# Recurrence of a hybrid block: a reordered step, and level matrices as 128x128 block diagonals

## The reference, cut to what matters

```python
def step(s, inp):                     # s: 64x64 state per direction and head
    r_t, w_t, k_t, v_t, aa_t, bb_t = inp
    sa = jnp.einsum('dbhij,dbhj->dbhi', s, aa_t)
    s = s * w_t[..., None, :] + sa[..., :, None] * bb_t[..., None, :] \
        + v_t[..., :, None] * k_t[..., None, :]
    y_t = jnp.einsum('dbhij,dbhj->dbhi', s, r_t)
    return s, y_t
```

## Time and profile before

| what | us |
|---|---|
| median of three runs (2741.93 to 2745.86) | 2744.94 |
| the profiled execution | 2746.3 |
| its span | 2744.5 |
| TensorE busy in the span | 2602.0 (95%) |
| VectorE, ScalarE, GpSimd busy | 960.9, 563.6, 148.3 |
| the recurrence, in the span | 1420.2 to 1667.4 |

### The profile page before, as it was taken

One profiled execution on the slowest core, in us unless ns is written; L12 is line 12 of the kernel. 1 busy time (PEld: TensorE's weight loads), 2 busy tenths in 40 slices (PEclk: granted clock), 3 DMA queues, 4 the chain that ended last, 5 costly groups with the idle time before them and its releaser, 6 DMA issues.

```text
span 2744.5 us, 42039 instructions
## 1 busy us (share of the span) xinstructions
PE 2602.0 (95%) x18006; PEld 1724.2 (63%) x18006; DVE 960.9 (35%) x1993; ACT 563.6 (21%) x1071; POOL 148.3 (5%) x125
## 2 busy tenths in 40 slices
PE   7999999998999999999998789799999999999998
PEld 6867878887885887888877777433333333333333
DVE  1773463312377254313576653411111111111112
ACT  2100233301100223301333323111111111111112
POOL 0050000000041000000012220000000000000000
PEclk9999999999999999999999999899999999999999
DMA  6645323343554432335400002599999999999995
GB/s 228 215 167 201 114 101 123 123 154 127 183 209 160 165 111 92 123 138 194 173 14 3 4 4 93 236 426 428 428 428 428 428 428 428 428 428 428 428 428 252
DMA packets 135044, 636.06 MB, mean 232 GB/s; under 512 B 5136, under 2 KB 5408, under 8 KB 109152
## 3 DMA queue, kind: packets, MB, share of 16 engines
q1 hardware_dynamic: 133904, 629.78, 57.8%
q0 software_dynamic: 1008, 4.30, 0.4%
HBM read 633.01 MB, written 1.05 MB: 231 GB/s over the span
## 4 chain that ended last, share of the span: by engine, by line
PE 92%; DVE 4%; ACT 3%; issue 1%; DMA 1%; SPq 0%; ACTq 0%; DVEq 0%
PE bank L265 25%; PE bank L2540 17%; PE bank L2568 9%; PE bank L455 6%; PE bank L1402 5%; PE bank L477 4%; PE bank L286 4%; PE bank L1337 4%; PE bank L2502 2%; PE bank L2531 2%; PE bank L2488 2%; PE bank L1624 1%; PE bank L353 1%; PE bank L2560 1%; ACT hidT L2650 1%
## 5 line engine op out<-in xcount | busy, mean ns | idle before, releaser
L265 PE MATMUL bank<-hT,ring 128*128 128x256 f32 x3136 | 694.7, 382 | 13.0 <-DVE hT L706 13.0
L265 PEld LDWEIGHTS bank<-hT,ring 128*128 128x128 f32 x3136 | 596.3, 191 | 106.8 <-DVE hT L706 14.8
L2540 PE MATMUL bank<-ring,hsel 128*64 128x512 f32 x2112 | 462.0, 595 | 0.0
L2540 PEld LDWEIGHTS bank<-ring,hsel 128*64 128x64 f32 x2112 | 149.0, 137 | 311.5 <-issue 311.5
L2812 DVE TENSOR_SCALAR glu<-bank 128x256 f32<-128x256 f32 x66 | 28.0, 425 | 761.0 <-PE bank L2540 757.7
L2568 PE MATMUL bank<-ring,hidT 128*64 128x512 f32 x1024 | 226.8, 595 | 22.0 <-ACT hidT L2650 22.0
L1402 PE MATMUL bank<-ring 64*64 64x64 f32 (+1 forms) x5760 | 179.9, 230 | 42.1 <-DVE ring L2136 19.0
L739 DVE SCALAR_TENSOR_TENSOR a_buf<-v_pad,par,a_buf 128x256 f32<-128x256 f32 x480 | 215.8, 532 | 0.0
L1402 PEld LDWEIGHTS bank<-ring 64*64 64x64 f32 x5760 | 168.1, 141 | 54.4 <-issue 19.7
L2568 PEld LDWEIGHTS bank<-ring,hidT 128*64 128x64 f32 x1024 | 70.7, 137 | 156.0 <-issue 127.9
L2641 ACT ACTIVATE sig<-glu 128x256 f32<-128x256 f32 x66 | 27.5, 417 | 463.6 <-DVE glu L2812 463.6
(11 more groups left out here) (421 smaller groups left out, 2491.3 us busy)
## 6 DMA issues: line engine op xcount, KB each, us to landing
ring<-in_w SPq DMA_DIRECT2D x196, 2048.0 KB, 15.5
ring<-in_w_in SPq DMA_DIRECT2D x66, 2048.0 KB, 7.9
ring<-in_w_ada SPq DMA_DIRECT2D x12, 2048.0 KB, 8.1
ring<-in_w_ret_out SPq DMA_DIRECT2D x8, 2048.0 KB, 7.9
ring<-in_w_out SPq DMA_DIRECT2D x6, 2048.0 KB, 8.0
ring<-in_w_conv_out SPq DMA_DIRECT2D x4, 2048.0 KB, 8.5
ring<-in_w_attn_out SPq DMA_DIRECT2D x4, 2048.0 KB, 7.8
extra<-in_w SPq DMA_DIRECT2D x2, 2048.0 KB, 25.3
```

What stands on the lines that cost most here:

```text
L265: mm = nc.tensor.matmul(out[:, j, :], w[:, k, col + j * P:col + (j + 1) * P], rhs[:, k, :], start=(k == 0), stop=(k == DC - 1))
L2540: mm = nc.tensor.matmul(half(flat[4 + b], side), g["hsel"][:, 2 * (j % 2) + k, j // 2, :], w[:, at:at + UNIT], start=False, stop=(j == 3 a ...
```

## The change

In `mixer_memory`, `cut` gets two buffers, each with a 128x128 matrix per direction and pair; MP loses its second half to a new MQ. GpSimd zeroes `cut` once, and then writes each level in four pieces: two directions, two halves of 64 partitions, each into its own block (for the backward direction the off-diagonal one). TensorE's first product of a level, `t1`, is one product of 128 rows instead of two halves. X0 is no longer formed by VectorE from MP: X1 is turned through the identity into PSUM (`turn_x1`), X0's updates accumulate there, and ScalarE copies X0 out after each level (`keep_x0`). The pairs and starts of the next turn (`front`) come ahead of the state products. The token turns go ahead of levels 1 to 3, the other products between `t1` and the second products (`between`). The number of waits falls: TensorE waits for both directions at once. The loras of the latent half go ahead of turn 0 and behind turns' ends. The expert stage only takes its counters from other, spent semaphores.

```diff
-    g["cut"] = flat[:, at:at + LEVELS * DN * C2].rearrange("p (k n w) -> p k n w", k=LEVELS, n=DN)
+    g["cut"] = flat[:, at:at + 2 * DN * P].rearrange("p (k n w) -> p k n w", k=2, n=DN)
...
                 if k == 0:
                     pool.wait_ge(g["pairs_out"].sem, g["pairs_out"].at(turn, d + 1))
-                nc.gpsimd.tensor_tensor(g["cut"][:, k, d * NC:(d + 1) * NC, :], g["MP"][:, d * NC:(d + 1) * NC, 0:C2],
-                                        row(mask[:, k, d, :], NC), ALU.mult).then_inc(
-                    g["levels_cut"].sem, g["levels_cut"].one())
+                elif k > 1:
+                    pool.wait_ge(g["t_done"].sem, g["t_done"].at(turn, 2 * (k - 1)))
+                for lo in (0, 64):
+                    to = 64 - lo if d else lo
+                    nc.gpsimd.tensor_tensor(
+                        g["cut"][lo:lo + 64, k % 2, d * NC:(d + 1) * NC, to:to + 64],
+                        g["MP"][lo:lo + 64, d * NC:(d + 1) * NC, :],
+                        mask[lo:lo + 64, k, d, :].unsqueeze(1).to_broadcast([64, NC, C2]), ALU.mult).then_inc(
+                        g["levels_cut"].sem, g["levels_cut"].one())
+    pool.wait_ge(g["p_out"].sem, g["p_out"].at(None, CTX_CHUNKS + 20))
+    nc.gpsimd.memset(g["cut"][:, :, :, :], 0.0).then_inc(g["wf_zero"].sem, g["wf_zero"].one())
...
+        def turn_x1(d, c):
+            for lo in (0, 64):
+                to = 64 - lo if d else lo
+                mm = nc.tensor.matmul(chunk(4 + d, c)[to:to + 64], g["XX"][lo:lo + 64, d, 1, c, :],
+                                      ident[lo:lo + 64, lo:lo + 64], start=c == 0, stop=False, skip_group_check=True)
+            return mm
+
+        def t1(k):
+            return lambda d, c: nc.tensor.matmul(chunk(d, c), g["cut"][:, k % 2, d * NC + c, :], g["XX"][:, d, 1, c, :],
+                                                 start=True, stop=True)
+
+        def d1(d, c):
+            return halves(chunk(2 + d, c), g["XX"][:, d, 0, c, :], g["T1"][:, d * NC + c, :], turned=d == 1)
+
+        def d0(k):
+            return lambda d, c: halves(chunk(4 + d, c), g["T1"][:, d * NC + c, :], g["XX"][:, d, 0, c, :],
+                                       False, k == LEVELS - 1)
...
+        def between(k):
+
+            if k == 0:
...
+                both_ways(keys, "pairs_done")
+            if k == 1:
...
+                if lat:
+                    both_ways(more, "more_done")
+                if turn == 2:
+                    lora(1, 3, 6)
+            if k == 2:
...
+                both_ways(g0_state, "g0_done", True)
+            if k == 3:
...
+                both_ways(g0_keys, "g0_done")
+            if k == 4:
...
+                if keep_state:
+                    both_ways(state_keys)
+                if lat:
+                    both_ways(out_state, "y_step", True)
+
+        for k in range(LEVELS):
+
+            if k == 0:
+                pe.wait_ge(g["x_ready"].sem, g["x_ready"].at(turn, 2))
+                both_ways(turn_x1, "x1_turned")
+            else:
...
+                if k < 4:
+                    both_ways(by_token(("sV", "sB", "sK")[k - 1]))
+                pe.wait_ge(g["x_next"].sem, g["x_next"].at(turn, 2 * k))
+            pe.wait_ge(g["levels_cut"].sem, g["levels_cut"].at(turn, 4 * k + 4))
+            both_ways(t1(k), "t_done")
+            between(k)
+            pe.wait_ge(g["t_out"].sem, g["t_out"].at(turn, 2 * k + 2))
...
+            if k < LEVELS - 1:
+                both_ways(d1, "d_done")
+            both_ways(d0(k), "x0_done")
+
+        pe.wait_ge(g["x0_out"].sem, g["x0_out"].at(turn, 2 * LEVELS))
+        both_ways(u, "u_done")
         if turn == 0:
...
+            key_sums(1, 2)
         if turn == 1:
...
+            lora(1, 2, 2)
+        if keep_state and turn != STEPS - 1:
+            front(turn + 1)
+        pe.wait_ge(g["u_out"].sem, g["u_out"].at(turn, 2))
         if keep_state:
...
+            both_ways(state_rates, "s_done")
...
         if lat:
...
+            both_ways(out_keys)
+            both_ways(out_rates, "y_step")
+        if turn == STEPS - 1:
+            front(turn + 1)
```

ScalarE and VectorE follow:

```diff
+        def keep_x0(k):
+            for d in range(DIRS):
+                act.wait_ge(g["x0_done"].sem, g["x0_done"].at(turn, 2 * k + d + 1))
+                nc.scalar.activation(g["XX"][:, d, 0].rearrange("p c w -> p (c w)"), flat[4 + d][:, 0:NC * C2], ACT.Copy).then_inc(
+                    g["x0_out"].sem, g["x0_out"].one())
+
         for k in range(LEVELS):
+            if k:
+                keep_x0(k - 1)
             for d in range(DIRS):
...
+    def start_inverse(turn):
+
+        dve.wait_ge(g["first_done"].sem, g["first_done"].at(turn, 1))
         for d in range(DIRS):
...
+            v.tensor_tensor(g["MP"][:, d * NC:(d + 1) * NC, :], flat[d][:, 0:NC * C2].rearrange("p (n w) -> p n w", n=NC),
+                            row(keep[:, d, 0:C2], NC), ALU.mult).then_inc(g["pairs_out"].sem, g["pairs_out"].one())
+        for d in range(DIRS):
+            x = g["XX"][:, d, 1]
+            v.tensor_tensor(x, flat[d][:, NC * C2:2 * NC * C2].rearrange("p (n w) -> p n w", n=NC), row(first[:, d, :], NC),
+                            ALU.mult).then_inc(g["starts_set"].sem, g["starts_set"].one())
+            dve.wait_ge(g["starts_set"].sem, g["starts_set"].at(turn, d + 1))
+            v.tensor_tensor(x, x, row(g["mc"]("eye"), NC), ALU.add).then_inc(g["x_ready"].sem, g["x_ready"].one())
...
+        start_inverse(turn)
+        if turn:
+            add_state(turn - 1)
...
+                    v.tensor_tensor(x, x, flat[2 + d][:, 0:NC * C2], ALU.add).then_inc(g["x_next"].sem, g["x_next"].one())
```

More of the change, by code:

```diff
@@ L1404, in halves, with both_ways, chunk, front @@
         return mm
-    def both_ways(product, last, signal, per_direction=False):
-        for c in range(last + 1):
+    def both_ways(product, signal=None, last_only=False):
+        for c in range(NC):
             for d in range(DIRS):
                 mm = product(d, c)
-                if signal and c == last and (d or per_direction):
+                if signal and c == NC - 1 and (d or not last_only):
                     mm.then_inc(g[signal].sem, g[signal].one())
[L1414 to L1432, removed]
+    ident = g["c"]("ident")
+    def chunk(bank, c, at=0):
+        return flat[bank][:, at + c * C2:at + (c + 1) * C2]
+    def front(turn):
+        def pairs(d, c):
+            dc = d * NC + c
+            return halves(chunk(d, c), g["sB"][:, dc, :], g["sA"][:, dc, 0:C2], turned=d == 1)
         def first(d, c):
             dc = d * NC + c
-            return halves(flat[4 + d][:, c * C2:(c + 1) * C2], g["sA"][:, dc, 0:C2], g["sB"][:, dc, :], turned=d == 1)
-        def by_token(name, bank, at):
+            return halves(chunk(d, c, NC * C2), g["sA"][:, dc, 0:C2], g["sB"][:, dc, :], turned=d == 1)
+        pe.wait_ge(g["staged"].sem, g["staged"].at(turn, 1))
+        both_ways(pairs)
+        both_ways(first, "first_done", True)
+    def step(turn):
+        lat, i = turn >= STEPS, turn % STEPS
+        state = g["ST"][turn % 2]
+        keep_state = turn < 2 * STEPS - 1
+        new_col = C2 * (1 + turn % 2)
+        def by_token(name):
             def product(d, c):
@@ L1537, in step @@
-        for d in range(DIRS):
-            pe.wait_ge(g["x_next"].sem, g["x_next"].at(turn, 2 * (LEVELS - 1) + d + 1))
-            for c in range(NC):
-                mm = halves(flat[d][:, c * C2:(c + 1) * C2], g["XX"][:, d, 0, c, :], g["G0"][:, d * NC + c, :])
-            mm.then_inc(g["u_done"].sem, g["u_done"].one())
+                    mm = nc.tensor.matmul(chunk(d, c, NC * C2)[to:to + 64], g[name][lo:lo + 64, d * NC + c, :],
+                                          ident[lo:lo + 64, lo:lo + 64], start=True, stop=True)
@@ L1559, in mixer_tensor @@
+    pe.wait_ge(g["p_out"].sem, g["p_out"].at(None, CTX_CHUNKS + 20))
+    pe.wait_ge(g["lora_out"].sem, g["lora_out"].at(None, 4))
+    lora(1, 0, 2)
+    lora(1, 1, 6)
+    front(0)
+    g["first_done"].n = 0
+    for turn in each_turn(g, 2 * STEPS, SCAN):
+        step(turn)
     pe.wait_ge(g["gates_ready"].sem, g["gates_ready"].at(None, 1))
@@ L1753, in aside @@
             key_exp(1)
-        if n in (14, 15):
-            take_lora(1, 2, 4, n - 14)
-        if n in (18, 19):
-            take_lora(1, 3, 4, n - 18)
+        if n == 23:
+            for part in range(2):
+                take_lora(1, 3, 6, part)
         if 25 <= n < 37:
@@ L2166, in step, with add_state @@
+    def add_state(turn):
         for d in range(DIRS):
@@ L2168, in step, with new_state @@
             h = slice(d * NC, (d + 1) * NC)
-            ins = v.tensor_tensor(g["sum"][:, h, :], old[:, h, :],
+            ins = v.tensor_tensor(g["sum"][:, h, :], g["ST"][turn % 2][:, h, :],
                                   flat[6 + d][:, 0:NC * C2].rearrange("p (n w) -> p n w", n=NC), ALU.add)
-        ins.then_inc(steps.sem, steps.one())
-        dve.wait_ge(steps.sem, steps.now(i))
```

(17 more changed lines are left out.)

388 lines of the change are left out of this document (162 added, 226 removed).

## The result

The changed kernel takes 2760.85 us (median of 4 runs, 2759.64 to 2764.93), the kernel before beside it on the same chip 2745.33 us (4 runs, 2741.93 to 2745.86). The ratio is 1.0062, 95% interval 1.0044 to 1.0079: slower by 15.5 us, where 2766 was forecast. The profiled execution has a span of 2759.0 us, against 2744.5.

The account below looks back on a forecast made before the run. TensorE bounds the kernel, and the 247.2 us recurrence moves the end one for one. Products +34, shape switches +8, d1 -15 give +27 us of work; less 6 of better covered waits, +21 on 2744.9: 2766 us, range 2741 to 2783.

Parts of the forecast that it names:

- The sign and the size: Recurrence stage +21 us, passed on in full to the end: 2766 us; slower by more than noise, chance 0.69.
- Rival 1: Each level's 16 first-product instructions not bound by weight loads, 0.058 us each: 34 us less, 2732 us; chance 0.14.
- First product: Each level: 16 whole-tile instructions at 0.111 us, 1.78 instead of 0.93 us; +0.85 per level, +34 us over 40.
- Switches: Shape changes between 64x64 and 128-column weights at each level: 0.2 us a level, +8 us; bounds 0 and 0.4.
- What the product is measured against: Baseline for each level's first product: today's 32 instructions, direction by direction, 0.93 us, giving +0.85 per level.
- Second products: X1's update d1 goes to fast order, 0.93 to 0.46 us, in four levels; X0's d0 stays slow: -15 us.
- The clock: Low granted clock after each step's starting wait: 1.0 us a latent step, 1.5 a context step, against 1.7 before.
- The steps at full clock: Latent step summed to 30.9 us at full clock, including 4.6 from front's end to the first product.
- Rival 2: Small losses don't come: switches preloaded (-8), no front stretch (-6), clock at 2.4 GHz (-8 to -11); 2743 us, chance 0.18.
- Rival 3: GpSimd bounds level 0: half pieces take 1.13 us, 1.6 us longer in 8 steps, +13: 2779 us; chance 0.14.
- Rival 4: Pipelining across the recurrence saves more waits than found and hides the products' price: 2735 us; chance 0.03.

Follow-up runs that it names:

- e1: Changed kernel with each level's first product as 64x64 quarters from the same block diagonals, directions alternating: 2718.96 us, ratio 0.9899.
- e7: Changed kernel plus few wide filling products in TensorE's idle time before the turning of x1: 2749.87 us, ratio 1.0016.
- e2: e1 with compact level matrices, ten whole GpSimd multiplications a turn, no zeroing and no buffer waits: 2710.59 us, ratio 0.9874.
- e3: Kernel before the change with the block diagonals alone (GpSimd pieces and whole-tile first product), old order kept: 2771.47 us, one run.
- e4: e1 with its first product direction by direction instead of alternating: 2724.11 us, one run.
- e9: e1 with the wide filling products of e7: 2722.19 us, ratio 0.9921.
- e10: e7 with X1's second product d1 direction by direction instead of alternating: 2749.45 us, ratio 1.0017.
- e6: e2 plus many small filling products (128 instructions a step, 64 in the last three) before the turning of x1: 2730.15 us, ratio 0.9939.
- e8: e2 with the wide filling products of e7: 2714.01 us, ratio 0.9886.

## Why the prediction was right, and where it wasn't

**The sign and the size.** Forecast +21 us, by 27 of work less 6 of better covered waits; measured +18 in the stage and +15.5 in the time, and TensorE's busy time rose by 25. The cause is the one named: take the whole-tile product away and the loss turns into a gain of 1% (e1). That the sum came within 3 us of the stage is in part luck, as the terms below show. And the sentence that nothing behind the stage absorbs what it loses did not hold to the microsecond: 18 us in the stage became 14.5 in the span, by the clock behind it. Rival 1 needed a spacing under 0.08 us.

**First product.** Taken at 0.111 us per instruction from rows with 32 moving columns. The 16 take 2.00 us at full clock; less 0.28 for the last one's own duration, over 15 steps, that is 0.115. Right, and 0.06 a level too little.

**Switches.** Taken at 0.2 us a level. In e7, where nothing else is waited for, the product's first start comes 0.15 us after the last start ahead of it, 0.12 more than usual, and the next group's 0.20 after the product's last, 0.09 more than its own spacing: 0.21 in all. Right. By the Trainium skill, "TensorEngine Tiling (Array Packing)", Key Properties, a change of mode drains the engine; the 0.4 a level that I had made of that rule, which has no price on the page, was twice too much.

**What the product is measured against.** This step was incomplete. I charged it +0.85 a level over the slow order of before, and booked the faster orders only for d1. In the new pipeline the alternative is 0.46 for the first product too; that is what e1 runs. The block diagonals, product and pieces, cost 50 us there (against e2) and 25 in the old order (e3, one run). Of the 25 us between them the slow order explains 2 to 5 (e4) and the clock 14 (e7, e9), if the two add up; the rest no run takes apart. The forecast's sum is not wrong by it, but it didn't say that the change is a gain of 35 us (e2) with a loss of 50 on top (42 for the product, 8 for GpSimd's pieces).

**Second products.** Term -15 for d1. e10 takes back only the alternation, not the other half for the backward direction: 4 us of TensorE's work, 2 in the stage, 0 in the time. The term put two things together; with the backward direction turned, the slow order takes 0.76 and not 0.93 (e4). Half of what alternation bought was given back as waiting for VectorE (5.2 us in e7, 3.0 in e10). How much of the 15 the other half brought, no run shows.

**The clock.** This step failed. I had 1.0 us a latent step and 1.5 a context step, 10 in all and less than the 1.7 a step of before, "since products now split the idle stretch". The fill shows 15.3 us in the stage, 1.9 a step (11.0 in the median times), and PEclk went down. The turning of x1, 0.7 us of work between two waits of 1.1 to 2.6 and 0.7 us, doesn't keep the clock; and what then runs at 1.2 GHz in part is the longest product of the level (2.94 us instead of 2.00) and the keys behind it.

**The steps at full clock.** Forecast 30.9 us for a latent one; the three of e7 from one level 0 to the next take 30.3, 30.0 and 29.7. Levels 0 to 3 were put at 19.4 and take 19.0, level 0 5.1 instead of 4.4 and the others less; the rest at 11.5 and takes 10.6 to 11.3. From front's end to the first product I had 4.6 us, of which 0.8 for VectorE's additions being stretched by GpSimd. It is 4.1: of the two additions of a step one takes 0.42 us and the other 0.50. The first matrix waits for GpSimd and not for them, and beside them the second and third of GpSimd's four pieces take 0.83 and 0.79 us instead of 0.72. The lock of the Trainium skill, "SBUF — State Buffer", Who interferes with whom, which I had weighed for the later value, can thus be worth 0.2 us a step here, not the 0.8 of the sum; in the kernel before, one of the two longer additions of a step took 1.10 us instead of 0.69. So this term was 0.5 us a step too long. It and the shorter steps made up for the clock; two errors of 5 to 8 us cancelled, which is luck.

**The rivals.** Of Rival 2's small losses the switches came in full, the clock's more than in full, the stretch at the front for the most part not. e7 is what its clock part gives, 2749.9 against the 2755 to 2758 of taking 8 to 11 us off the forecast. Rival 3: the pieces on GpSimd take 0.76 us in the mean and 1.07 at most, not 1.13, hold the first product of level 0 up by 0.6 us a step, and cost 8 us in all, but they don't bound the level. Rival 4: the pipelining does save more than I had found, 35 us (e2), but it doesn't hide the product. Its gain was counted too low, and the interaction with the product too.

## What to carry to other kernels

Price an instruction against the best alternative in the new order, not against what stands there now: the pipelining alone was worth 1.3%, and the block diagonals took more than that. Zeros in a weight matrix were not free here: a level's eight whole-tile products, of two 64x64 blocks each, took 2.00 us where the sixteen 64x64 products, in turn over four quarters, took 0.70. Where an idle stretch precedes the longest product of a chain, look at the granted clock behind it, and if you fill the idleness, fill it with few wide instructions; where small products with waits of their own follow, as in e1 and e2, the fill gained nothing.

## What the runs showed of the hardware

TensorE can stop without waiting for any engine that the profile shows. Dense 64x64 products (33 matmuls and as many weight loads a microsecond in e2's recurrence, waits included) stop for 0.2 to 1.3 us there, and for up to 1.9 us in e6, about every 128 matmuls and about once for each 16 KB packet of the instruction queue; the profile calls it a wait with the releaser "issue". That the supply of instructions is the cause is argued from this distance and from e6 and e8, not shown. In e2 that is 25.6 us of 217, and it may be what bounds that kernel now; fewer, larger instructions for the same work would be the way to try. The Trainium skill, "Advanced Engine Details and Errata", Sequencer and Instruction Queues, begins with the sequencer reading the next instruction; what that read can cost the page does not say, and whether the stops above are that read no run here shows.

Filling TensorE's idle time with work that nobody reads made the changed kernel 11 us faster; the granted clock was 0.91 in its recurrence without the fill and 1.00 with it.
